# Moving operands read and sums written backwards in all projections, with an offset for each stage

## The chip, the cores and the metric

One core of one Trainium2 chip. The metric is the device time of the whole kernel in microseconds. The kernel before took 1453.62 us (median of three runs, 1452.39 to 1457.54).

## What is computed

Three transformer-like blocks on a sequence of 256 tokens, width 1024, everything in float32. The first block runs retention and a gated linear recurrence side by side, then a gated feed-forward layer of width 3072; each of the two layers of the second part runs a feed-forward layer (width 2816), a mixer (gated linear attention, convolution, windowed attention) and a second feed-forward layer. Cut to what takes the time, the projections:

```python
proj = h @ w_in[l]                                     # 1024 x 8192
y_a = (o * silu(g_ret)) @ w_ret_o[l]                   # 1024 x 1024
y_b = (hl * gelu(y_lru)) @ w_lru_o[l]                  # 1024 x 1024
x = x + mix @ w_out[l]                                 # 1024 x 1024
up = h @ ffn_w_up[l]                                   # 1024 x 6144
x = x + (gelu(gate) * val) @ ffn_w_down[l]             # 3072 x 1024
# and for each of two layers, twice a feed-forward layer and once the mixer:
h = (silu(h @ w_gate) * (h @ w_up)) @ w_down           # 1024 x 2816 twice, 2816 x 1024
p = h @ w_in                                           # mixer, 1024 x 2064
h = concatenate([o_gla, o_conv, o_swa]) @ w_out        # 1024 x 1024
```

## The kernel before

**Splitting.** Each float32 operand of a projection is split into two parts of type fp32r: ScalarE copies the rounded high part, VectorE subtracts it and writes the low part. A product is then three matmuls into the same sums: high by high, high by low, low by high. fp32r matmuls take one column per step; other matmuls in the kernel (transposes, attention, convolution taps) are full float32.

**Weights.** They come in 240 units of 1 MB (128 partitions x 2048 values) through three slots: SyncE issues the loads into `raw`, ScalarE writes `w_hi` (L632), VectorE writes `w_lo` (L1028), TensorE uses both. A slot is filled anew when its unit has been split and split anew when TensorE has used it.

**Activations.** The projections' other operand lies in `a_pair` or `b_pair`: one stretch of 2 x 8 x 256 values per partition, high part first, low part behind it, with 128 values to spare. `operand_pair` (L223) takes the pair out of that stretch from a column `at`, which the tables `A_AT` and `B_AT` (L130, L131) give for each stage: `N_IN` the first input projections, `N_LRU` the recurrence's output projection, `N_UP1` the first up projection, `N_F`, `N_L + 1`, `N_L + 2`, `N_L + 4` the four feed-forward layers of the second part, `N_L` and `N_L + 3` the two mixers; `B_RG` the block-diagonal gates, `B_RETO` the retention's output projection, `B_OUT` the first block's output projection, `B_MIX` the mixers' output projections. A column is 4 bytes. The down projections read `h_hi` and `h_lo` instead, which no table moves.

**Two widths.** `feature_major` (and `token_major`, for one unit of each mixer) issues matmuls of 256 moving columns: in `feature_major` the moving operand is the activation and the stationary one 128 x 128 of the weights, 48 matmuls for each unit. `wide_pass` and `deep_pass` issue matmuls of 512 moving columns: the moving operand is the weights, the stationary one 128 x 128 of the activation. Feature-major are the first block's input projections (but the values), gates, retention and recurrence outputs and the up projection, and most of the mixers' input projections; all else is wide.

**Order.** TensorE's program is written out by hand: unit after unit, with small work (transposes, scores, variances) put between or inside them. Each matmul instruction brings its own weight load, which runs beside the matmul before it. All matmuls go through the helper `mm` (L1713), so they have one line in the profile; sums go to PSUM banks named `stream`, `psm` and `ps7` (shown as `ps`).

Of the kernel before, what the change touches and what calls it, by code (L numbers as in the profile page):

```python
# [26 lines left out]
TT = T // P  # L27
D = 1024
KT = D // P
# [97 lines left out]
(N_LRU, N_IN, N_UP1, N_F, N_L) = (-2, -1, 0, 1, 2)  # L127
NORMS = N_L + 3 * LAYERS
B_RG, B_RETO, B_OUT, B_MIX = range(4)
A_AT = {N_IN: 4, N_LRU: 16, N_UP1: 16, N_F: 0, N_L: 16, N_L + 1: 0, N_L + 2: 0, N_L + 3: 16, N_L + 4: 0}  # L130
B_AT = {B_RG: 16, B_RETO: 16, B_OUT: 0, B_MIX: 0}  # L131


def root_count(i, post, t):
# [69 lines left out]
def build(nc, io, out):  # L204
    with ExitStack() as ctx:  # L205
# [30 lines left out]
        a_hi, a_lo = a_tiles(N_IN)  # L236
        raw = [sb(f"raw{s}", [P, KT, UC]) for s in range(NS)]
        w_hi = [sb(f"w_hi{s}", [P, KT, UC], F32R) for s in range(NS)]
        w_lo = [sb(f"w_lo{s}", [P, KT, UC], F32R) for s in range(NS)]
# [148 lines left out]
        def y_bank(t, n):  # L388

            return psm[:, 2 * t + n, :]  # L390
# [1317 lines left out]
        def _(pe):  # L1708
            passed = {"n": 0}
            a_hi, a_lo = a_tiles(N_IN)  # L1710

            def mm(dst, lhs, rhs, start, stop):
                return nc.tensor.matmul(dst, lhs, rhs, start=start, stop=stop, skip_group_check=True)  # L1713

            def split_unit(c):
                pe.wait_ge(w_split, c + 1)

# [6 lines left out]
            def feature_major(s, dst, tiles, hi_t, lo_t, first, last, kts=range(KT), ready=None):  # L1724

                for n, (lhs, at) in enumerate(tiles):  # L1730
                    for k in kts:
                        if ready and n == 0:
                            ready(k)
                        to = dst[:, at:at + T]
                        begin, end = first and n == 0 and k == kts[0], last and n == len(tiles) - 1 and k == kts[-1]
                        mm(to, lhs(w_hi[s], k), hi_t[:, k, :], begin, False)
                        mm(to, lhs(w_hi[s], k), lo_t[:, k, :], False, False)
                        ins = mm(to, lhs(w_lo[s], k), hi_t[:, k, :], False, end)
                return ins

            def block_cols(f):
# [4 lines left out]
            def token_major(s, dst, col, width, at, begin, a_hi, a_lo, tiles=range(TT), ready=None):  # L1746

                for t in tiles:
                    to = dst[:, at + t * width:at + t * width + width]
                    tok = slice(t * P, t * P + P)  # L1750
                    for k in range(KT):
                        w = slice(col, col + width)
                        if ready:
                            ready(k)
                        mm(to, a_hi[:, k, tok], w_hi[s][:, k, w], begin and t == 0 and k == 0, False)
                        mm(to, a_lo[:, k, tok], w_hi[s][:, k, w], False, False)
                        ins = mm(to, a_hi[:, k, tok], w_lo[s][:, k, w], False, t == TT - 1 and k == KT - 1)
                return ins

            def wide_pass(c, t, dst, hi_t, lo_t, ks, first, last, ready=None):  # L1760

                split_unit(c)
                tok = slice(t * P, t * P + P)
                h, l = wide(w_hi[c % NS]), wide(w_lo[c % NS])
                for n, k in enumerate(ks):
                    if ready:
                        ready(k)
                    begin, end = first and n == 0, last and n == len(ks) - 1
                    mm(dst, hi_t[:, k, tok], h[:, n, :], begin, False)
                    mm(dst, hi_t[:, k, tok], l[:, n, :], False, False)  # L1770
                    ins = mm(dst, lo_t[:, k, tok], h[:, n, :], False, end)
                end_pass(ins, c, t)

            def deep_pass(c, t, hi_t, lo_t, ks, first, last, ready, between):

                split_unit(c)
                tok = slice(t * P, t * P + P)
                h, l = deep(w_hi[c % NS]), deep(w_lo[c % NS])
                for n in range(2):
                    cols = slice(512 * n, 512 * n + 512)  # L1780
                    for j, k in enumerate(ks):
                        if (n, t) == (0, 0):
                            ready(k)
                        mm(y_bank(t, n), hi_t[:, k, tok], h[:, j, cols], first and j == 0, False)
                        mm(y_bank(t, n), hi_t[:, k, tok], l[:, j, cols], False, False)
                        ins = mm(y_bank(t, n), lo_t[:, k, tok], h[:, j, cols], False, last and j == 1)
                        if n + j == 2:
                            end_pass(ins, c, t)
                        elif last and (n, j) == (0, 1):
                            ins.then_inc(half_done, 1)  # L1790
                        if between[2 * n + j]:
                            between[2 * n + j]()
# [33 lines left out]
            for k in range(KT):  # L1826
                for t in range(TT):
                    at = (k % 2) * T + t * P
                    ins = nc.tensor.transpose(psm[:, k // 2, at:at + P], x_t[:, t, k * P:k * P + P], ident)
# [21 lines left out]
            for u in range(8):  # L1851
                if u < 4:
                    project(u, u, stream[u % 3], a_hi, a_lo, (lambda k: pe.wait_ge(a_split, k + 1)) if u == 0 else None)
                else:
                    n, m = divmod(u - 4, 2)
# [418 lines left out]
```

## Time and profile before

| | |
|---|---|
| median of three runs | 1453.62 us |
| the profiled execution's own time | 1452.81 us |
| its span, first to last instruction | 1450.9 us |
| TensorE matmul busy | 1423.1 us (98%), 8888 matmuls |
| weight loads busy | 1247.8 us, 8888 loads |
| VectorE, ScalarE, GpSimd busy | 968.7, 735.9, 94.5 us |
| granted TensorE clock, mean | 0.998 |
| DMA | 259 MB, 179 GB/s |

Times in the profile are microseconds unless marked ns. PE is TensorE's matmuls, PEld its weight loads, DVE is VectorE, ACT ScalarE, POOL GpSimd. A group of instructions reads: line, engine, operation, output <- inputs, sizes (stationary rows * columns, moving partitions x columns), count, then busy time and the mean duration of one in ns, then the idle time of the engine just before them and who ended it. Busy time is a union, so overlapping matmuls count once. The ends of matmuls are modelled; their starts are recorded, so the distance between starts is the sure number.

### The profile page before, as it was taken

Reading aid. Unit: us, or ns where it says so; the run is one execution under the profiler, and the core shown is the slowest. Engines: PE = TensorE matmul, PEld = TensorE weight load, DVE = VectorE, ACT = ScalarE, POOL = GpSimd, SP = SyncE. Lnnn points to the kernel's source line nnn. Section 1 sums busy time; section 2 is a strip of 40 time slices with the busy share of each in tenths; the row PEclk is TensorE's granted clock in tenths of the full one; section 3 lists DMA queues with packets and bytes.
Section 4 is the critical chain, followed back from the end, with each engine's and each line's share of the span. In section 5 each row is a group of like instructions: output and inputs, shape, how many; then the busy total and the mean of one; then the engine's idle time right before and its main releaser. Section 6 shows DMA issues by size and latency. Waiting matters only on the chain. (4 is left out here: it accounts for less than half of the span.)

```text
span 1450.9 us, 21310 instructions
## 1 busy us (share of the span) xinstructions
PE 1423.1 (98%) x8888; PEld 1247.8 (86%) x8888; DVE 968.7 (67%) x1165; ACT 735.9 (51%) x936; POOL 94.5 (7%) x107
## 2 busy tenths in 40 slices
PE   7999999999999999999999999999999999999998
PEld 7899999899988788888987888878888898788886
DVE  5968786688864665546977665556665579665644
ACT  5534854555643544446656444454444567544442
POOL 0001000000000000001720000000000045000000
PEclk9999999999999999999999999999999999999999
DMA  7745455667655666456334755547754462466542
GB/s 244 232 139 182 158 191 198 176 191 201 198 192 163 211 210 224 153 193 159 133 114 143 221 174 189 189 146 246 231 186 171 140 174 103 138 198 197 178 161 101
DMA packets 251411, 259.13 MB, mean 179 GB/s; under 512 B 26659, under 2 KB 213428, under 8 KB 251316
## 3 DMA queue, kind: packets, MB, share of 16 engines
q1 hardware_dynamic: 250432, 255.49, 55.5%
q10 hardware_dynamic: 884, 2.28, 0.4%
q8 instruction: 70, 1.15, 0.3%
q14 instruction: 25, 0.20, 0.0%
HBM read 256.69 MB, written 1.05 MB: 178 GB/s over the span
## 5 line engine op out<-in xcount | busy, mean ns | idle before, releaser
L1028 DVE TENSOR_TENSOR w_lo<-raw,w_hi 128x2048 fp32r<-128x2048 f32 x240 | 548.2, 2287 | 317.5 <-ACT w_hi L632 317.1
L632 ACT ACTIVATE w_hi<-raw 128x2048 fp32r<-128x2048 f32 x240 | 456.3, 1902 | 332.0 <-PE psm L1713 150.8
L1713 PE MATMUL stream<-a_pair,w_hi 128*128 128x256 f32 x2144 | 378.2, 280 | 3.5 <-DVE a_pair L1047 1.9
L1713 PE MATMUL stream<-w_hi,a_pair 128*128 128x512 f32 (+1 forms) x1152 | 363.4, 388 | 8.1 <-DVE w_lo L1028 5.7
L1713 PEld LDWEIGHTS stream<-a_pair,w_hi 128*128 128x128 f32 x2144 | 325.9, 188 | 6.1 <-issue 3.3
L1713 PE MATMUL stream<-a_pair,w_lo 128*128 128x256 f32 x1072 | 298.4, 278 | 0.0
L1713 PEld LDWEIGHTS stream<-w_hi,a_pair 128*128 128x128 f32 x1152 | 214.2, 188 | 53.2 <-DVE w_lo L1028 8.3
L1713 PE MATMUL stream<-w_lo,a_pair 128*128 128x512 f32 (+1 forms) x576 | 221.0, 384 | 0.0
L1713 PEld LDWEIGHTS stream<-a_pair,w_lo 128*128 128x128 f32 x1072 | 201.8, 188 | 0.0
L1713 PE MATMUL psm<-w_hi,h_hi 128*128 128x512 f32 x448 | 175.1, 391 | 0.0
L1713 PE MATMUL psm<-w_hi,h_lo 128*128 128x512 f32 x448 | 174.4, 389 | 0.0
L1713 PE MATMUL psm<-w_lo,h_hi 128*128 128x512 f32 x448 | 174.3, 389 | 0.0
L1713 PEld LDWEIGHTS stream<-w_lo,a_pair 128*128 128x128 f32 x576 | 108.3, 188 | 20.1
L1713 PE MATMUL ps<-w_hi,a_pair 128*128 128x512 f32 x320 | 105.5, 391 | 0.0
L1713 PEld LDWEIGHTS psm<-w_hi,h_lo 128*128 128x128 f32 x448 | 84.1, 188 | 17.6
L1713 PEld LDWEIGHTS psm<-w_lo,h_hi 128*128 128x128 f32 x448 | 84.1, 188 | 17.3
L1713 PEld LDWEIGHTS psm<-w_hi,h_hi 128*128 128x128 f32 x448 | 84.1, 188 | 17.1
L552 POOL TENSOR_TENSOR rs<-var,mhalf 128x1 f32<-128x1 f32 x28 | 15.2, 544 | 1135.8 <-DVE var L1074 1104.5
L1713 PEld LDWEIGHTS ps<-w_hi,a_pair 128*128 128x128 f32 x320 | 60.1, 188 | 12.4
L856 ACT ACTIVATE gu<-stream,rs 128x256 f32<-128x256 f32 x68 | 32.2, 474 | 72.8 <-PE stream L1713 72.8
L1713 PE MATMUL psm<-w_hi,b_pair 128*128 128x512 f32 x192 | 63.0, 398 | 1.1 <-DVE b_pair L1035 1.1
L1713 PE MATMUL ps<-w_lo,a_pair 128*128 128x512 f32 x160 | 62.3, 389 | 0.0
(278 smaller groups left out, 1361.0 us busy)
## 6 DMA issues: line engine op xcount, KB each, us to landing
raw<-in_ffn_w_up SPq DMA_DIRECT2D x136, 512.0 KB, 5.0
raw<-in_ffn_w_down SPq DMA_DIRECT2D x104, 512.0 KB, 4.4
raw<-in_ffn_w_gate SPq DMA_DIRECT2D x88, 512.0 KB, 4.0
raw<-in_w_in SPq DMA_DIRECT2D x80, 512.0 KB, 4.7
raw<-in_w_out SPq DMA_DIRECT2D x24, 512.0 KB, 4.3
raw<-in_w_ret_o SPq DMA_DIRECT2D x8, 512.0 KB, 4.5
raw<-in_w_lru_o SPq DMA_DIRECT2D x8, 512.0 KB, 4.3
diag<-in_conv_diag SPq DMA_DIRECT2D x8, 512.0 KB, 5.8
```

What stands on the lines that cost most here:

```text
L552: nc.gpsimd.tensor_tensor(to, of, mhalf[:, 0:1].broadcast_to([P, n]), ALU.pow).then_inc(rstd_ready, 1)
L632: nc.scalar.activation(w_hi[s][:, :, 0:n], raw[s][:, :, 0:n], ACT.Copy).then_inc(w_hi_ready, 1)
L856: nc.scalar.activation(th_t[:, 2 * (g % 2) + t, :], up_bank(g, t)[:, 0:UC], ACT.Tanh, scale=rs4[:, 2 + t:3 + t]).then_inc(th_ready, 1)
L1028: V.tensor_tensor(w_lo[s][:, :, 0:n], raw[s][:, :, 0:n], w_hi[s][:, :, 0:n].bitcast(F32), ALU.subtract).then_inc(w_split, 1)
L1713: return nc.tensor.matmul(dst, lhs, rhs, start=start, stop=stop, skip_group_check=True)
```

## The change

It adds a helper, `backward`, which hands `mm` the output and the moving operand with their columns in reverse order; the stationary operand stays as it is. The four functions that issue projections call it for each of their three matmuls. Since the moving operand and the sums are both reversed, each sum lands where it did. The two tables of offsets get new values. Nothing else differs.

```diff
-A_AT = {N_IN: 4, N_LRU: 16, N_UP1: 16, N_F: 0, N_L: 16, N_L + 1: 0, N_L + 2: 0, N_L + 3: 16, N_L + 4: 0}
-B_AT = {B_RG: 16, B_RETO: 16, B_OUT: 0, B_MIX: 0}
+A_AT = {N_IN: 32, N_LRU: 64, N_UP1: 48, N_F: 16, N_L: 16, N_L + 1: 32, N_L + 2: 48, N_L + 3: 8, N_L + 4: 24}
+B_AT = {B_RG: 16, B_RETO: 40, B_OUT: 64, B_MIX: 0}
...
+            def backward(to, of, moving, begin, end):
+
+                return mm(to[:, ::-1], of, moving[:, ::-1], begin, end)
+
...
-                        mm(to, lhs(w_hi[s], k), hi_t[:, k, :], begin, False)
-                        mm(to, lhs(w_hi[s], k), lo_t[:, k, :], False, False)
-                        ins = mm(to, lhs(w_lo[s], k), hi_t[:, k, :], False, end)
+                        backward(to, lhs(w_hi[s], k), hi_t[:, k, :], begin, False)
+                        backward(to, lhs(w_hi[s], k), lo_t[:, k, :], False, False)
+                        ins = backward(to, lhs(w_lo[s], k), hi_t[:, k, :], False, end)
...
-                    mm(dst, hi_t[:, k, tok], h[:, n, :], begin, False)
-                    mm(dst, hi_t[:, k, tok], l[:, n, :], False, False)
-                    ins = mm(dst, lo_t[:, k, tok], h[:, n, :], False, end)
+                    backward(dst, hi_t[:, k, tok], h[:, n, :], begin, False)
+                    backward(dst, hi_t[:, k, tok], l[:, n, :], False, False)
+                    ins = backward(dst, lo_t[:, k, tok], h[:, n, :], False, end)
```

`token_major` and `deep_pass` are changed in the same way.

## Rows read from the trace of the kernel before

**Rows 1.** The page: busy us by engine, share of the span, instructions.
```profile
PE 1423.1 (98%) x8888; PEld 1247.8 (86%) x8888; DVE 968.7 (67%) x1165; ACT 735.9 (51%) x936; POOL 94.5 (7%) x107
```

**Rows 2.** The page, granted TensorE clock in tenths, the span in 40 slices.
```profile
PEclk9999999999999999999999999999999999999999
```

**Rows 3.** Waits, whole span: who waited for whom, total us, times, longest.
```profile
ACT w_hi L632 <- PE psm L1713: 150.8, 51, 4.4
ACT w_hi L632 <- PE stream L1713: 114.0, 36, 6.3
...
ACT w_hi L632 <- PE ps L1713: 53.8, 20, 3.5
...
PE stream L1713 <- DVE w_lo L1028: 6.3, 10, 1.3
```

**Rows 4.** Groups of matmuls by form, whole span; first and last of each width.
```profile
L1713 PE MATMUL stream<-a_pair,w_hi 128*128 128x256 f32 x2144 | 378.2, 280 | 3.5 <-DVE a_pair L1047 1.9 <-DVE a_pair L1066 1.1 <-DVE w_lo L1028 0.6
L1713 PE MATMUL stream<-w_hi,a_pair 128*128 128x512 f32 x1088 | 351.9, 394 | 5.7 <-DVE w_lo L1028 5.7
...
L1713 PE MATMUL psm<-w_lo,a_pair 128*128 128x512 f32 x32 | 12.6, 395 | 0.0
...
L1713 PE MATMUL stream<-w_lo,a_pair 128*128 128x256 f32 x32 | 8.9, 279 | 0.0
```

**Rows 5.** Groups by form, 280 to 400 us, the first up projection.
```profile
L1713 PE MATMUL stream<-a_pair,w_hi 128*128 128x256 f32 x708 | 120.5, 276 | 0.0
L1713 PE MATMUL stream<-a_pair,w_lo 128*128 128x256 f32 x354 | 97.7, 276 | 0.0
```

**Rows 6.** Groups by form, 99 to 122 us, the first input projections.
```profile
L1713 PE MATMUL stream<-a_pair,w_hi 128*128 128x256 f32 x133 | 23.4, 279 | 0.0
L1713 PE MATMUL stream<-a_pair,w_lo 128*128 128x256 f32 x67 | 18.7, 278 | 0.0
```

**Rows 7.** Timeline of matmuls in a mixer: start us, length us, what, count.
```profile
689.91 0.28 PE L1713 MATMUL stream<-a_pair,w_lo 128*128 128x256 f32 x1
...
690.97 0.28 PE L1713 MATMUL stream<-a_pair,w_lo 128*128 128x256 f32 x1
```

**Rows 8.** Groups by form, 1405 to 1445 us, the last down projection.
```profile
L1713 PE MATMUL psm<-w_lo,h_hi 128*128 128x512 f32 x60 | 23.3, 389 | 0.0
L1713 PE MATMUL psm<-w_hi,h_lo 128*128 128x512 f32 x59 | 23.0, 389 | 0.0
L1713 PE MATMUL psm<-w_hi,h_hi 128*128 128x512 f32 x59 | 23.0, 389 | 0.0
```

**Rows 9.** Timeline of matmuls, the first stage of 512 columns.
```profile
60.25 0.39 PE L1713 MATMUL psm<-w_lo,a_pair 128*128 128x512 f32 x1
...
61.65 0.39 PE L1713 MATMUL psm<-w_lo,a_pair 128*128 128x512 f32 x1
```

**Rows 10.** Timeline of matmuls around a pause in the first input projections.
```profile
123.27 0.28 PE L1713 MATMUL stream<-a_pair,w_lo 128*128 128x256 f32 x1
...
125.36 0.28 PE L1713 MATMUL stream<-a_pair,w_lo 128*128 128x256 f32 x1
125.99 1.05 PE L1713 MATMUL ps<-keep,sq 128*128 128x1 f32 x8 [0.35 <-POOL sq L569]
...
127.23 0.28 PE L1713 MATMUL stream<-a_pair,w_lo 128*128 128x256 f32 x1
...
128.93 0.28 PE L1713 MATMUL stream<-a_pair,w_lo 128*128 128x256 f32 x1
```

**Rows 11.** The page, weight loads of the largest group.
```profile
L1713 PEld LDWEIGHTS stream<-a_pair,w_hi 128*128 128x128 f32 x2144 | 325.9, 188 | 6.1 <-issue 3.3
```

**Rows 12.** Timeline of matmuls, convolution taps in full float32.
```profile
731.77 2.11 PE L1713 MATMUL ps<-up,diag 128*128 128x256 f32 x9
```

## What I expect, and why

> **What bounds the kernel now.** I read the busy times first: TensorE is busy 1423.1 of 1450.9 us, VectorE 968.7 [rows 1]. Then the clock: every slice of the span has the full grant, so all durations below are at 2.4 GHz [rows 2]. Then who waits for whom. The dearest wait of TensorE's matmuls is 6.3 us in all, for the low half of a weight unit, while ScalarE waits 150.8, 114.0 and 53.8 us for TensorE to free a weight slot [rows 3]. So nothing feeds TensorE late: the kernel is a chain of matmuls, and the change acts on the matmuls alone. What counts is no instruction's duration (these overlap and their ends are modelled) but the distance from one start to the next.
>
> The projections come in two widths: 3600 matmuls of 256 moving columns, in six groups, and 3840 of 512, in eleven; the first and the last group of each width are shown [rows 4]. At one column per cycle they would take 3600 x 106.7 ns = 384 us and 3840 x 213.3 ns = 819 us. I get the real distances by counting matmuls in a stretch that holds nothing else (the length plus one duration, over the count, since matmuls that reach into the stretch are counted):
> - the first block's up projection: (120 + 0.276) us / (708 + 354) = 113.3 ns [rows 5]
> - the input projections, g_ret and y_lru: (23 + 0.279) / (133 + 67) = 116.4 ns [rows 6]
> - the mixer: nine matmuls from 689.91 to 690.97, 117.8 ns [rows 7]
> - down projections, 512 columns: (40 + 0.389) / (59 + 59 + 60) = 226.9 ns [rows 8]
> - the first stage's 512 columns: six matmuls from 60.25 to 61.65, 233.3 ns [rows 9].
>
> Two losses are to be seen. **One is everywhere and goes with the columns:** 113.3 and 226.7 ns are 272 and 544 cycles, 17 for every 16 columns. **The other comes and goes:** 3 to 5 ns on a 256 matmul, 6.6 ns on a 512 one in the first stage. It isn't set by addresses alone. The first block's up projection and the mixer read their operand at the same offset (16) and differ by 4.5 ns. And in one stage at one offset the distance changes at a pause: 18 matmuls from 123.27 to 125.36 stand 116.1 ns apart, then eight matmuls of one column come in, and the 15 from 127.23 to 128.93 are 113.3 apart [rows 10]. So it depends on where two streams stand to each other in time. The second stream is the weight load: there is one for every matmul (2144 loads for the 2144 of that group), 188 ns long [rows 11], beside the running matmul.
>
> **The change, part by part.** It adds and removes no instruction, no wait and no transfer. The queues of SyncE, ScalarE, VectorE and GpSimd keep their order; ScalarE and VectorE write operand tiles of the same sizes, from 32 bytes before to 256 bytes behind their old places. (1) All 7440 projection matmuls read their moving operand from the last column down; (2) they write PSUM in the same descending order, so what lands is the same; (3) the operand pair starts at another offset in ten of the thirteen stages; the block-diagonal gates (16), the first mixer's projections (16) and the mixers' output projections (0) keep theirs. The 256-wide passes have the operand pair as moving side, the 512-wide ones as stationary side, so an offset shifts one stream against the other in both.
>
> *Cost of reading and writing downward.* No row shows a matmul that does this. Bound below: the loss per 16 columns goes. The nearest row is the convolution's taps, full float32, which take two cycles per column and show no such loss: (2.11 - 0.38) us / 8 = 216.3 ns for 256 columns, 3 ns over 2 x 106.7 [rows 12]. By them 512 columns would take 213.3 + 3 = 216.3 and 256 columns 109.7. That is at most 3840 x (226.9 - 216.3) = 41 us and, from a mean of (1152 x 113.3 + 2448 x 116.9) / 3600 = 115.7 ns, 3600 x 6.0 = 22 us: -63 us in all. Bound above: the two cycles per column of those same rows, if a downward stream is not served at one column per cycle: 3840 x (429 - 227) + 3600 x (216 - 116) = +1136 us. I take zero: the loss is the same 1 in 16 for both widths, whatever the roles and however much of the matmul the 188 ns load covers, so it looks like a property of the stream itself, and nothing in the rows gives a stream a preferred direction.
>
> *Worth of the offsets and of the direction against the weight load.* This acts on the second loss. Of the 3600 matmuls, 24 units x 48 = 1152 are the up projection, already at 113.3. The other 2448 stand between 113.3 and 117.8; I take 116.9 for them, the middle of the slow rows (116.1 to 117.8) [rows 6, 7, 10]. If all reach 113.3: 2448 x 3.6 = 8.8 us. The first stage's 96 wide matmuls: 96 x (233.3 - 226.7) = 0.6 us. Sum -9.4 us. If nothing changes: 0. If it turns out worse, see the third rival. I take the whole -9.4: each slow stage gets another offset or at least, with the direction, another meeting of its two streams, two streams that run the same way pass over each other more slowly than two that meet, and the low value is one that every kind of 256 stage is seen to reach. That is a choice, not a derivation.
>
> *What is late next.* A PE that is 9 us faster over the whole asks for each weight unit under 1% sooner; ScalarE's 318.6 us of waiting for slots [rows 3] hides that. Even the 63 us of the lower bound fit: it is 5 to 6% on each unit. I let 5 us return as waits in that case.
>
> **Sum.** The profiled execution took 1452.8 us, span 1450.9 plus 1.9 around it; the median of the three timed ones is 1453.6, 0.8 above. 1452.8 - 9.4 = 1443.4; I say 1443.
>
> **The rules of the Trainium skill.** The skill's page TensorE: Matmul & The Clock Gate, section Back-to-back issue gap, gives N/2.4 + 2.5 ns. The 227 and 113 ns of rows 5 and 8 disagree with it, the measurement decides for this kernel; by the rule the wide matmuls would be at 215.8, which is the first rival's result. The same page (Step-by-step) says that PE has two independent SBUF read ports, so a weight load takes no bandwidth from the running matmul. By that rule the offsets do nothing and the sum is 0; rows 10, with 116.1 and 113.3 ns on either side of a pause, speak against it without proving that the port is the cause. The page Advanced Engine Details and Errata, section PSUM Cachelines, speaks against this change: any non-contiguous pattern slows matmuls significantly, and two consecutive elements should be contiguous. Descending neighbours are still neighbours, so I hold it unlikely; if the hardware counts them as non-contiguous, the last rival follows. No row here has a stepped PSUM write.
>
> **The rivals.**
> 1. *The 1 in 16 goes as well.* For it: the taps, which stream at half the rate beside the same loads, don't have it [rows 12], and the extra cycles are whole multiples of 16 (16, 32, and 48 in the first stage's 233.3), as if the load's passes were counted too. Against it: half of a 512 matmul lies beyond its load, and still has its share. It gives 1452.8 - 63 + 5, less or more as it goes in part: 1390 to 1430, most likely 1395.
> 2. *Nothing changes by direction or offset*, or gains in some stages pay for losses in others: 1447 to 1460.
> 3. *Two streams in the same direction stay on each other.* They part at half the speed of the moving one, so where they meet they meet for longer. Place: every weight load. Price: the wide stages, now without the second loss, get the first stage's 233.3: 3744 x 6.4 = 24 us; the up projection gets 117.8: 1152 x 4.5 = 5 us; +29 us, 1482. It decides once a quarter of the wide matmuls (1140 x 6.4 = 7.3 us) is hit with nothing gained elsewhere. For it: the up projection and the wide stages stand at their best now, and can only lose.
> 4. *A downward stream or write isn't served at full rate*: from +5% up to the +1136 us above, about 2590.
>
> **How the numbers follow.** Forecast (1438 to 1447) 0.34, of which 0.06 is a gain under 0.5%. Rival 1: 0.21. Rival 2: 0.20. Rival 3: 0.17, of which 0.02 within 0.5%. Rival 4: 0.08. A measurement of this kernel tells about 0.5% (7 us) from no change. Faster 0.28 + 0.21 = 0.49; same 0.06 + 0.20 + 0.02 = 0.28; slower 0.15 + 0.08 = 0.23. For the range I leave out rival 4 (0.08), the far part of rival 1 (0.06) and of rival 3 (0.04): 1392 to 1484. The forecast's own range is 1438 to 1447.
>
> **What would show it.** In the changed profile: the same 8888 matmuls; the up projection still with 1062 matmuls in 120 us, the down projections with 178 in 40 us; the mixer's nine matmuls in 1.02 us, not 1.06; the first stage's six in 1.36, not 1.40. If 1 in 16 goes, the 40 us hold 187 wide matmuls. If streams stay on each other, 173. A mean matmul duration of 276 or 389 ns that grows by 3 to 6 is the second loss. The prediction is wrong if the wide stages, 3840 matmuls that I leave untouched, move by more than 1 ns each.

## The result: about 2% slower

The changed kernel takes 1483.72 us (median of three runs, 1482.76 to 1485.72) against 1453.62: a ratio of 1.020, 95% interval 1.0176 to 1.0223. So it is slower for sure; whether by more or less than 2% stays open. The forecast was 1443. In the later comparisons the kernel before had 36 executions with medians of 1457.5 to 1458.5 us, four of them under 1454; beside 1458.4 the changed kernel is 1.7% slower. The profiled execution took 1485.72 us, with a span of 1483.9.

Busy times and granted clock, from the page of the changed kernel (compare [rows 1, 2]):

```profile
PE 1458.3 (98%) x8888; PEld 1262.3 (85%) x8888; DVE 968.6 (65%) x1165; ACT 736.6 (50%) x936; POOL 94.0 (6%) x107
...
PEclk9999999999999999999999999999999999999999
```

Only TensorE grew: 1458.3 against 1423.1 us, 35.2 more, for a span 33.0 longer. The clock is the same in every slice. The waits of ScalarE for a weight slot (compare [rows 3]; total us, times, longest) grew with it, so TensorE is still the engine that everything waits for:

```profile
ACT w_hi L632 <- PE psm L1713: 163.4, 53, 4.4
ACT w_hi L632 <- PE stream L1713: 119.5, 37, 6.5
```

The distances, by the same counting as before. Groups by form in 290 to 410 us, the first up projection (compare [rows 5]):

```profile
L1713 PE MATMUL stream<-a_pair,w_hi 128*128 128x256 f32 x668 | 120.3, 282 | 0.0
L1713 PE MATMUL stream<-a_pair,w_lo 128*128 128x256 f32 x335 | 94.5, 282 | 0.0
```

(120 + 0.282) / (668 + 335) = 119.9 ns, where it was 113.3. In 100 to 123 us, the first input projections (compare [rows 6]):

```profile
L1713 PE MATMUL stream<-a_pair,w_hi 128*128 128x256 f32 x129 | 23.3, 283 | 0.0
L1713 PE MATMUL stream<-a_pair,w_lo 128*128 128x256 f32 x65 | 18.4, 283 | 0.0
```

(23 + 0.283) / 194 = 120.0 ns, where it was 116.4. The first mixer, timeline of matmuls (start us, length us; compare [rows 7]):

```profile
709.79 0.28 PE L1713 MATMUL stream<-a_pair,w_lo 128*128 128x256 f32 x1
...
710.87 0.28 PE L1713 MATMUL stream<-a_pair,w_lo 128*128 128x256 f32 x1
```

Nine matmuls in 1.08 us, 120.0 ns apart, where it was 117.8. The last down projection, 1430 to 1470 us (compare [rows 8]):

```profile
L1713 PE MATMUL psm<-w_hi,h_lo 128*128 128x512 f32 x58 | 23.0, 397 | 0.0
L1713 PE MATMUL psm<-w_hi,h_hi 128*128 128x512 f32 x58 | 23.0, 397 | 0.0
L1713 PE MATMUL psm<-w_lo,h_hi 128*128 128x512 f32 x57 | 22.6, 397 | 0.0
```

(40 + 0.397) / 173 = 233.5 ns, where it was 226.9. And the first stage of 512 columns (compare [rows 9]):

```profile
60.80 0.40 PE L1713 MATMUL psm<-w_lo,a_pair 128*128 128x512 f32 x1
...
61.51 0.40 PE L1713 MATMUL psm<-w_lo,a_pair 128*128 128x512 f32 x1
```

Three matmuls in 0.71 us, 236.7 ns, where it was 233.3.

So no stage gained. In the down projections 226.7 to 233.3 ns is 544 to 560 cycles, in the up projection 113.3 to 120.0 is 272 to 288: 16 cycles for each matmul. The other stages rose by less.

The bill, from the mean distance of neighbouring starts in every stage of both traces: the wide matmuls rose from 227.5 to 233.4 ns on average, 3840 x 5.9 = 22.7 us; the up projection gives 1152 x 6.7 = 7.7 us; the other 2448 matmuls of 256 columns rose by 2.2 ns on average, 5.4 us. Together 35.8 us, and the busy time grew by 35.2. Least moved the retention's output projection (116.7 to 117.8), the recurrence's (117.8 to 118.3) and the second mixer (117.3 to 117.8).

### The profile page after: what moved, and what is told of

It reads as the page before. It is cut to its first block and busy times, and to the rows that moved or that the text cites. A ratio compares the mean times of both kernels' runs of the same rounds, so it can differ in the third digit from the quotient of the medians.

```text
span 1483.9 us, 21310 instructions
## 1 busy us (share of the span) xinstructions
PE 1458.3 (98%) x8888; PEld 1262.3 (85%) x8888; DVE 968.6 (65%) x1165; ACT 736.6 (50%) x936; POOL 94.0 (6%) x107
## 5 line engine op out<-in xcount | busy, mean ns | idle before, releaser
L1713 PE MATMUL stream<-a_pair,w_hi 128*128 128x256 f32 x2144 | 390.0, 284 | 2.8 <-DVE a_pair L1047 1.5
L1713 PE MATMUL stream<-w_hi,a_pair 128*128 128x512 f32 (+1 forms) x1152 | 370.2, 394 | 7.5 <-DVE w_lo L1028 5.2
L1713 PEld LDWEIGHTS stream<-a_pair,w_hi 128*128 128x128 f32 x2144 | 330.5, 188 | 5.1 <-issue 2.9
L1713 PE MATMUL stream<-a_pair,w_lo 128*128 128x256 f32 x1072 | 303.1, 283 | 0.0
L1713 PE MATMUL stream<-w_lo,a_pair 128*128 128x512 f32 (+1 forms) x576 | 224.9, 390 | 0.0
L1713 PE MATMUL psm<-w_hi,h_hi 128*128 128x512 f32 x448 | 178.7, 399 | 0.0
L1713 PE MATMUL psm<-w_lo,h_hi 128*128 128x512 f32 x448 | 178.1, 397 | 0.0
L1713 PE MATMUL psm<-w_hi,h_lo 128*128 128x512 f32 x448 | 178.0, 397 | 0.0
```

## The experiments

The runs e3 to e15 are one execution each, and executions of one kernel lie up to 9 us apart here, so in them the distances between starts count and not the time. A count of matmuls in 40 us is good to one matmul, 1.3 ns. Where a mean over a whole stage is given, it is that of the distances of neighbouring starts.

Each edit is given against the changed kernel, whose helper is `backward`, unless it says otherwise. "Offsets of before" means the two tables of the kernel before.

### Direction or offsets?

Theory D: the direction costs 16 cycles, at any offset. Theory O: the new offsets cost.

```diff
 e1_down_old_offsets
-A_AT = {N_IN: 32, N_LRU: 64, N_UP1: 48, N_F: 16, N_L: 16, N_L + 1: 32, N_L + 2: 48, N_L + 3: 8, N_L + 4: 24}
-B_AT = {B_RG: 16, B_RETO: 40, B_OUT: 64, B_MIX: 0}
+A_AT = {N_IN: 4, N_LRU: 16, N_UP1: 16, N_F: 0, N_L: 16, N_L + 1: 0, N_L + 2: 0, N_L + 3: 16, N_L + 4: 0}
+B_AT = {B_RG: 16, B_RETO: 16, B_OUT: 0, B_MIX: 0}
```

> Everything as in the changed kernel, but with the offsets of the kernel before. If the direction alone costs (theory D: 16 cycles more for each weight load, at any offset): 512-column matmuls 233.3 ns apart, 256-column ones 120.0, time 1480 to 1490. If the new offsets cost (theory O): 226.7 and 113 to 118 ns, time within 5 us of the kernel before. A mixture: some stages at 227, some at 233.

Measured: 1487.25 us, ratio 1.0204 (1.0182 to 1.0226) to the kernel before beside it. The down projections hold 173 matmuls in 40 us, 233.5 ns, the up projection 1002 in 120, 120.0 ns. With the old offsets the whole loss is there: theory D, but for one stage. The first stage's wide matmuls, at offset 4, stand 233.3 ns apart in e1 (six from 60.19 to 61.59 us), as in the kernel before. Where the ascending matmul stood at 233.3 already, the direction adds nothing; it is no fixed surcharge.

```diff
 e2_up_new_offsets (against the kernel before)
-A_AT = {N_IN: 4, ...
-B_AT = {B_RG: 16, ...
+A_AT, B_AT of the changed kernel
```

> Ascending as in the kernel before, with the new offsets. Theory D: down projections 226.7 ns, up projection of the first block 113.3, the first stage's wide matmuls 226.7 (offset 32 columns in place of 4), time 1448 to 1458. Theory O: 1480 to 1490, 233.3 and 120.0 ns.

Measured: 1466.35 us, ratio 1.0061 (1.0040 to 1.0082). Up and down projections as D wants (113.3 and 226.9 ns). But not everything: the time lies over D's 1458, and the first stage's wide matmuls, expected at 226.7, have a mean of 232.4. Timeline of the first feed-forward layer of the second part, whose stationary operand went from offset 0 to 16:

```profile
521.42 0.40 PE L1713 MATMUL ps<-w_lo,a_pair 128*128 128x512 f32 x1
...
522.12 0.39 PE L1713 MATMUL ps<-w_lo,a_pair 128*128 128x512 f32 x1
```

Three matmuls in 0.70 us: 233.3 ns, ascending. In the kernel before the same stage stood at 226.7 (six from 519.70 to 521.06). Here only the stationary operand has moved, the moving one (the weights) lies where it lay. So an ascending matmul can be brought to the descending one's distance by a bad offset, and the new offsets cost 0.6% of their own. In the changed kernel they add nothing to the direction: e1 isn't faster than the changed kernel, and this stage, at the same offset 16, stands at 233.3 there too (six from 520.62 to 522.02).

### The read or the write?

Theory R: the descending read costs; theory W: the descending write.

```diff
 e3_read_down_only
-                return mm(to[:, ::-1], of, moving[:, ::-1], begin, end)
+                return mm(to, of, moving[:, ::-1], begin, end)
 e4_write_down_only
-                return mm(to[:, ::-1], of, moving[:, ::-1], begin, end)
+                return mm(to[:, ::-1], of, moving, begin, end)
```

> The moving operand is read from the last column down, the sums are written upward, so the columns of each output stand in the wrong order; all else as in the changed kernel. If the descending read costs (theory R, a meeting of two SBUF reads): 233.3 and 120.0 ns, 1480 to 1490 us. If the descending write to PSUM costs (theory W): 226.7 and 113 to 118 ns, about 1454 us. If both are needed: in between.

Measured: 1482.85 us in one execution. Down projections, groups by form in 40 us:

```profile
L1713 PE MATMUL psm<-w_hi,h_lo 128*128 128x512 f32 x58 | 23.1, 397 | 0.0
L1713 PE MATMUL psm<-w_hi,h_hi 128*128 128x512 f32 x58 | 23.1, 397 | 0.0
L1713 PE MATMUL psm<-w_lo,h_hi 128*128 128x512 f32 x58 | 23.0, 397 | 0.0
```

(40 + 0.397) / 174 = 232.2 ns (one matmul more or less in the count is 1.3 ns; the mean over the stage is 233.3). The up projection holds 682 + 340 matmuls in 120 us, 117.7 ns, where the changed kernel has 119.9 at the same offset. That is 2.5 us, within the 3 us that the changed kernel's own executions span, so it isn't shown that the downward write has a part in it.

> The opposite: read upward, written downward, output columns in the wrong order. Theory R: 226.7 and 113 to 118 ns, about 1454 us. Theory W: 233.3 and 120.0 ns, 1480 to 1490 us.

Measured: 1463.42 us, beside 1466.35 for e2, which has the same offsets and writes upward. The same 40 us:

```profile
L1713 PE MATMUL psm<-w_hi,h_hi 128*128 128x512 f32 x60 | 23.4, 389 | 0.0
L1713 PE MATMUL psm<-w_lo,h_hi 128*128 128x512 f32 x59 | 23.0, 389 | 0.0
L1713 PE MATMUL psm<-w_hi,h_lo 128*128 128x512 f32 x59 | 23.0, 389 | 0.0
```

(40 + 0.389) / 178 = 226.9 ns. In the up projection (120 + 0.276) / (707 + 354) = 113.4 ns. The read pays for the wide matmuls, and the write alone costs nothing at either width.

### Is it the weight load beside it?

Theory L: the cost comes from the load, by its columns. Theory S: once per descending matmul. Theory M, on the ascending loss: it goes with the moving columns. All four have the offsets of before.

```diff
 e5_up_64_weights, e6_down_64_weights (n = 128 for the first matmul into its sums, 64 for the others)
-                return mm(to[:, ::-1], of, moving[:, ::-1], begin, end)
+                return mm(to[0:n, :], of[:, 0:n], moving, begin, end)                 # e5
+                return mm(to[0:n, ::-1], of[:, 0:n], moving[:, ::-1], begin, end)     # e6
 e7_up_one_weight, e8_down_one_weight
+                return mm(to, of[:, 0:1].broadcast_to([P, P]), moving, begin, end)                     # e7
+                return mm(to[:, ::-1], of[:, 0:1].broadcast_to([P, P]), moving[:, ::-1], begin, end)   # e8
```

> Ascending, offsets of before; every projection matmul but the first into its sums takes only 64 of the 128 stationary columns, so half of the rows of sums stay unfinished. The weight loads are half as long, the moving columns as many. If the loss of 1 in 16 belongs to the moving columns (theory M): 512 columns still 226.7 ns apart, 256 columns 113.3. If it is caused by the weight loads (theory L, 32 cycles for each load of 128 beside a 512-column matmul and 16 beside a 256-column one): half of it, 220.0 and 110.0 ns.

> Descending read and write, offsets of before, 64 of the 128 stationary columns as in the run beside it. Against that run: if the descending read pays 16 cycles for each load of 128 columns, by the columns loaded (theory L), the extra halves to 8 cycles, 3.3 ns: 230.0 ns under theory M for the rest. If it pays 16 cycles once per matmul, however short the load (theory S, a start-up cost of a descending stream): 6.7 ns, 233.3 and 120.0 ns.

Measured: e5 1464.34 us, e6 1481.15. In e5 the loads take 134 ns in place of 188 and the down projections' matmuls stand *further* apart, 176 in 40 us: (40 + 0.392) / 176 = 229.5 ns, and the up projection's too, (120 + 0.278) / 1031 = 116.7. Neither theory had that. In e6, 40 us of the down projections:

```profile
L1713 PE MATMUL psm<-w_lo,h_hi 128*64 128x512 f32 x58 | 23.0, 396 | 0.0
L1713 PE MATMUL psm<-w_hi,h_lo 128*64 128x512 f32 x57 | 22.6, 396 | 0.0
L1713 PE MATMUL psm<-w_hi,h_hi 128*64 128x512 f32 x56 | 22.2, 396 | 0.0
L1713 PE MATMUL psm<-w_hi,h_hi 128*128 128x512 f32 x2 | 0.8, 398 | 0.0
```

(40 + 0.396) / 173 = 233.5 ns: the full descending distance with half the load. Not theory L. The up projection, though, is at (120 + 0.282) / 1016 = 118.4 ns, not at theory S's 120.0.

> Ascending, offsets of before; the stationary operand is one column repeated 128 times, so the weight load has its full length but stays at one address in each partition (the sums are those of that column). Control for the next run. Theory M: 226.7 and 113.3 ns. If the weight load's sweep over addresses causes the loss of 1 in 16: fewer, towards 216 and 109 ns.

> The same with the descending read and write. If the extra comes from two streams that sweep SBUF the same way (my third rival's mechanism): the extra 6.7 ns is gone or changed, 226.7 and 113 to 117 ns. If it belongs to the descending read itself (theory S): 233.3 and 120.0 ns as in the changed kernel.

Measured: e7 1466.84 us, e8 1480.16. e7, ascending, the load at one address, 40 us of the down projections:

```profile
L1713 PE MATMUL psm<-w_hi,h_lo 128*128 128x512 f32 x58 | 22.9, 394 | 0.0
L1713 PE MATMUL psm<-w_hi,h_hi 128*128 128x512 f32 x58 | 22.9, 394 | 0.0
L1713 PE MATMUL psm<-w_lo,h_hi 128*128 128x512 f32 x58 | 22.9, 394 | 0.0
```

(40 + 0.394) / 174 = 232.2 ns (the mean over that stage is 231.7), and the up projection is at (120 + 0.278) / 1031 = 116.7: theory M misses both. The same stage of e8, descending, then its up projection:

```profile
L1713 PE MATMUL psm<-w_hi,h_lo 128*128 128x512 f32 x58 | 23.0, 397 | 0.0
L1713 PE MATMUL psm<-w_hi,h_hi 128*128 128x512 f32 x58 | 23.0, 397 | 0.0
L1713 PE MATMUL psm<-w_lo,h_hi 128*128 128x512 f32 x57 | 22.6, 397 | 0.0
```

```profile
L1713 PE MATMUL stream<-a_pair,w_hi 128*128 128x256 f32 x681 | 120.4, 279 | 0.0
L1713 PE MATMUL stream<-a_pair,w_lo 128*128 128x256 f32 x341 | 95.1, 279 | 0.0
```

(40 + 0.397) / 173 = 233.5 and (120 + 0.279) / 1022 = 117.7 ns. For 512 columns the descending distance is the same with a whole load, half a load and a load that doesn't move. The ascending one changes with each: 226.9, 229.5, 232.2. So what the load does matters to an ascending matmul, and beside its own ascending control the direction costs 6.6, 4.0 and 1.3 ns: what is constant is the distance of 560 cycles, not the extra. For 256 columns the descending distance itself changes with the load: 120.0 in e1, which has the same offsets, 118.4 and 117.7, and the means of the other 256-column stages go the same way (119.7 to 120.0 in e1, 118.3 to 118.9 in e6, 117.8 to 118.1 in e8). There theory S fails.

### Columns and the order of blocks

Theory S again (16 cycles once), theory C: the extra goes by columns. Then, whether the cost lies in the order of columns inside 64 bytes or in the order of the blocks; these two write upward.

```diff
 e9_up_384, e10_down_384 (offsets of before; n = all columns for the first matmul into its sums, 3/4 of them for the others)
+                return mm(to[:, 0:n], of, moving[:, 0:n], begin, end)                       # e9
+                return mm(to[:, 0:n][:, ::-1], of, moving[:, 0:n][:, ::-1], begin, end)     # e10
 e11_blocks_down, e12_inside_down (offsets of before)
+                m = moving.rearrange("p (a b) -> p a b", b=16)
+                return mm(to, of, m[:, ::-1, :], begin, end)      # e11
+                return mm(to, of, m[:, :, ::-1], begin, end)      # e12
```

> Ascending, offsets of before; every projection matmul but the first into its sums moves three quarters of its columns (384 of 512, 192 of 256), the rest of the sums stays unfinished. If the ascending loss goes by columns (1 in 16): 384 columns take 384 x 17/16 = 408 cycles = 170.0 ns. If it is a fixed 32 cycles per matmul: 416 cycles = 173.3 ns.

> Descending read and write, three quarters of the columns as in the run beside it. If the descending read adds 16 cycles once per matmul (theory S): 408 + 16 = 424 cycles, 176.7 ns. If it adds by columns (1 in 32, so 3 in 32 in all; theory C): 384 x 35/32 = 420 cycles, 175.0 ns. 256-column form, now 192: S gives 204 + 16 = 220 cycles, 91.7 ns; but there the weight load of 107 ns is longer and should set the distance, so this form tells little.

Measured: 1282.32 and 1283.80 us. With a quarter of the columns gone TensorE waits for VectorE here and there, so I read the distances inside a down projection, six matmuls each. e9:

```profile
569.81 0.33 PE L1713 MATMUL psm<-w_hi,h_hi 128*128 128x384 f32 x1
...
570.85 0.33 PE L1713 MATMUL psm<-w_hi,h_hi 128*128 128x384 f32 x1
```

1.04 us / 6 = 173.3 ns, 416 cycles: 32 over the 384 columns, as many as for 512. e10:

```profile
565.90 0.34 PE L1713 MATMUL psm<-w_hi,h_hi 128*128 128x384 f32 x1
...
566.97 0.34 PE L1713 MATMUL psm<-w_hi,h_hi 128*128 128x384 f32 x1
```

1.07 / 6 = 178.3 ns, 428 cycles (the mean over the stages is 177.8, 427 cycles): 10 to 12 more than ascending. Both of my figures for e10 were built on 408 and miss; against the measured 416, S would be 432 and C 428. C fits better, but 256 columns also pay 16, so neither is a law. The narrower form, 192 columns, stands at 112.0 ns in either direction, (20 + 0.274) / 181 from 300 to 320 us in e9 and (120 + 0.275) / 1074 from 280 to 400 us in e10: here the direction costs nothing. What falls for sure is my loss of 1 in 16: it is 32 cycles at 512 and at 384 columns and 16 at 256.

> Ascending write, offsets of before; the moving operand is read in blocks of 16 columns (64 bytes), the last block first, upward inside each block. If the cost sits in the step from one column to the one below it inside a block: none here, 226.7 ns. If it sits in the step from a block to the one before it, or in where the matmul starts reading: 233.3 ns. A jump of 31 columns after every 16 may have a price of its own, then over 233.3.

> The other way round: blocks of 16 in ascending order, each read from its last column down. If the cost sits inside the blocks: 233.3 ns. If it sits in the order of blocks or in the start at the far end: 226.7 ns.

Measured: e11 1485.03 us, 233.5 ns in the down projections and (120 + 0.284) / 1002 = 120.0 ns in the up projection: all of the descending cost, with every 16 columns read upward. Whether it is the order of the blocks or the jump from each to the next that costs, this run can't tell. e12 1639.26 us, the slowest of all:

```profile
1599.72 0.43 PE L1713 MATMUL psm<-w_hi,h_hi 128*128 128x512 f32 x1
...
1601.32 0.43 PE L1713 MATMUL psm<-w_hi,h_hi 128*128 128x512 f32 x1
```

Six matmuls in 1.60 us, 266.7 ns, 640 cycles: one extra cycle for every four columns, in either width (133.4 ns for 256, 320 cycles). But not in every stage. The first input projections of e12, whose operand starts at offset 4, 16 bytes past a multiple of 64, in 100 to 123 us:

```profile
L1713 PE MATMUL stream<-a_pair,w_hi 128*128 128x256 f32 x130 | 23.4, 281 | 0.0
L1713 PE MATMUL stream<-a_pair,w_lo 128*128 128x256 f32 x64 | 18.0, 281 | 0.0
```

(23 + 0.281) / 194 = 120.0 ns. So the high price hangs on where the blocks start in SBUF: 133.3 ns in all the 256-column stages at offset 16, 117 to 120 in the only one at 4. Elsewhere the price of the plain descending read is that of its blocks' order; the order inside them costs nothing when the blocks descend too, and much when they ascend.

### One descending matmul among ascending ones, and a moving operand that doesn't move

```diff
 e13_one_of_three_down (against the kernel before; the third matmul of each three)
-                        ins = mm(to, lhs(w_lo[s], k), hi_t[:, k, :], False, end)
+                        ins = mm(to[:, ::-1], lhs(w_lo[s], k), hi_t[:, k, ::-1], False, end)
 e14_up_one_column (offsets of before)
+                return mm(to, of, moving[:, 0:1].broadcast_to([P, moving.shape[1]]), begin, end)
 e15_down_at_4
+A_AT = {N_IN: 4, N_LRU: 12, N_UP1: 4, N_F: 2, N_L: 20, N_L + 1: 6, N_L + 2: 12, N_L + 3: 28, N_L + 4: 40}
+B_AT = {B_RG: 12, B_RETO: 4, B_OUT: 20, B_MIX: 0}
```

> Offsets of before; of each three matmuls only the third reads and writes downward. If each descending matmul pays its own 16 cycles: the mean of three is 226.7 + 6.7/3 = 228.9 ns for 512 columns, time about 1466. If the cost sits in the change from one matmul's stream to the next (the place where one read ends and the next begins), two of three changes now differ from both pure kernels: up to 231 to 233 ns, time 1475 or more.

Measured: 1465.62 us. Groups by form, 40 us of the down projections; the third of three is the one from `h_lo`:

```profile
L1713 PE MATMUL psm<-w_hi,h_lo 128*128 128x512 f32 x59 | 23.4, 396 | 0.0
L1713 PE MATMUL psm<-w_hi,h_hi 128*128 128x512 f32 x59 | 23.0, 390 | 0.0
L1713 PE MATMUL psm<-w_lo,h_hi 128*128 128x512 f32 x59 | 23.0, 389 | 0.0
```

(40 + 0.392) / 177 = 228.2 ns, and the mean duration is 396 ns for the descending ones beside 390 and 389 for the others. Each descending wide matmul pays by itself, 6 to 7 ns by the durations; the changes of direction cost nothing to be seen. The up projection doesn't follow: (120 + 0.28) / (681 + 341) = 117.7 ns, two thirds of the way from 113.3 to 120.0 with one matmul of three descending. As this stage takes 117.7 in some ascending kernels too (e18 below), the run can't say what one such matmul costs there.

> Ascending write, offsets of before; the moving operand is one column repeated, so the moving read stays at one address (the sums are those of that column). If the 32 cycles that even an ascending 512-column matmul loses come from the moving read's way through SBUF: near 213.3 + 3 = 216 ns, as the convolution taps suggest. If they come with any fp32r matmul: 226.7 ns.

Measured: 1400.17 us. Down projections, groups by form in 35 us, then the up projection in 120 us:

```profile
L1713 PE MATMUL psm<-w_hi,h_lo 128*128 128x512 f32 x55 | 20.8, 379 | 0.0
L1713 PE MATMUL psm<-w_hi,h_hi 128*128 128x512 f32 x55 | 20.8, 379 | 0.0
L1713 PE MATMUL psm<-w_lo,h_hi 128*128 128x512 f32 x54 | 20.5, 379 | 0.0
```

```profile
L1713 PE MATMUL stream<-a_pair,w_hi 128*128 128x256 f32 x718 | 120.3, 275 | 0.0
L1713 PE MATMUL stream<-a_pair,w_lo 128*128 128x256 f32 x359 | 98.7, 275 | 0.0
```

(35 + 0.379) / 164 = 215.7 ns and (120 + 0.275) / 1077 = 111.7 ns. With the moving operand read at one place, the wide matmul's loss of 32 cycles is down to 6. And the loss that comes and goes is gone: every stage stands at 215.7 to 215.9 or at 111.7 ns, by its width, whatever its offset. Both losses need a moving read that moves. The 111.7 ns are, to 0.3 ns, the distance of 192 columns in e9 and e10; so in this run something other than the columns sets it. The weight load is the likely one, but no run shows it.

> Descending as in the changed kernel, with offsets that aren't multiples of 8 columns (2, 4, 6, 12, 20, 28; one at 40). If no offset helps a descending read, as the nine offsets tried so far suggest: every wide stage at 233.3 ns or above, 1480 to 1490 us. If the offsets were the missing piece (a phase difference that is no multiple of 8): at least one up stage at 226.7 ns.

Measured: 1487.15 us, 233.5 ns in the down projections; 233.3 or more in every wide stage and 119 to 120 ns in every 256-column stage. No offset tried frees the descending read.

### Offsets for the ascending kernel

```diff
 (against the kernel before; B_MIX stays at 0)
 e16_up_at_64   every entry of A_AT and B_AT 64
 e17_up_48      N_IN, N_LRU, N_UP1, N_L, N_L + 3, B_RG, B_RETO: 48, the others 0
 e18_up_16      the same entries 16, the others 0
```

> Ascending, every operand pair at offset 64 but the mixers' output projection (0). Ascending wide stages stood at 227 ns at offset 0 and 64 and at 229 to 234 at 4, 16, 24, 32, 48. If multiples of 64 columns (256 bytes) are the good places: all wide stages 226.7, the first one too (-0.6 us). The 256-column stages: 113.3 to 118 ns, unknown at 64 (the recurrence's output stood at 120.0 there). Time within 6 us of the kernel before, either way.

Measured: 1465.20 us, ratio 1.0049 (1.0035 to 1.0064). Wide matmuls of the first stage, timeline:

```profile
60.66 0.39 PE L1713 MATMUL psm<-w_lo,a_pair 128*128 128x512 f32 x1
...
61.34 0.39 PE L1713 MATMUL psm<-w_lo,a_pair 128*128 128x512 f32 x1
```

Three in 0.68 us, 226.7 ns, down from 233.3 at offset 4, as expected. But the up projection, 290 to 400 us:

```profile
L1713 PE MATMUL stream<-a_pair,w_hi 128*128 128x256 f32 x612 | 110.2, 283 | 0.0
L1713 PE MATMUL stream<-a_pair,w_lo 128*128 128x256 f32 x307 | 86.9, 283 | 0.0
```

(110 + 0.283) / 919 = 120.0 ns at offset 64, ascending. The place that suits a stationary operand is the worst seen for a moving one. Both bounds of the expectation were missed: 120.0 for 118, and 6.8 us for 6.

> Ascending; every stage of 256-column matmuls at offset 48, every wide stage but the first at 0. The first up projection stood at 113.3 ns at 16 and at 48, at 120.0 at 64. If the offset decides: all 256-column stages near 113.3, the 2448 slow ones gain up to 3.6 ns each, 1446 to 1452. If the stage's history decides, as at the pause in the kernel before: a mixture of 113 to 120 and a time within 6 us of the kernel before.

Measured: 1450.80 us, ratio 0.9951 (0.9936 to 0.9965): the best kernel of this study, 0.5% faster than the kernel before and 2.2% than the changed one. A piece of the first mixer:

```profile
699.98 0.28 PE L1713 MATMUL stream<-a_pair,w_lo 128*128 128x256 f32 x1
...
700.66 0.28 PE L1713 MATMUL stream<-a_pair,w_lo 128*128 128x256 f32 x1
```

Six matmuls in 0.68 us, 113.3 ns, where it was 117.8 at offset 16. The up projection holds (120 + 0.276) / 1061 = 113.4 ns. The means over the whole of the two mixers are 114.3 and 114.6, where they were 117.3. The first block's input projections and gates stay at 116 to 118, its retention and recurrence outputs at 117.8. So it is a mixture: the offset alone doesn't decide.

> The same with 16 in place of 48, which differs from the kernel before in the first input projections alone (16 for 4). If the offset decides: those 1152 matmuls go from 117 to 113.3 ns, -4 us. If history decides: 116 to 118 ns, no change that can be measured.

Measured: 1458.29 us, ratio 1.000 (0.999 to 1.001). The up projection, which has its old offset, 280 to 400 us:

```profile
L1713 PE MATMUL stream<-a_pair,w_hi 128*128 128x256 f32 x681 | 120.4, 279 | 0.0
L1713 PE MATMUL stream<-a_pair,w_lo 128*128 128x256 f32 x341 | 95.1, 279 | 0.0
```

(120 + 0.279) / 1022 = 117.7 ns, at the same offset at which the kernel before has 113.3: for 1152 x 4.4 = 5 us. The two kernels differ in nothing but the offset of an earlier stage, but it isn't shown that this offset is the cause. All ten executions of e18 took 1457.5 to 1459.1 us, and so, to 0.4 us, did thirteen of the fourteen of the kernel before beside them; the fourteenth took 1452.2, like the profiled one. So more likely most executions of the kernel before have the up projection at 117.7 too, and the stage takes one distance or the other by something that changes between executions. That is argued: none of the slower ones was profiled. It would also account for e17's gain: 5 us in the up projection and 816 x 2.9 = 2.4 us in the mixers are the 7.5 us between the medians, while between the two profiled executions there are 2.4.

## Why the prediction was wrong

**What bounds the kernel** was right: the clock, the waits and the other engines are as they were, and the change went one to one into the time.

**The step that failed** is the cost of reading downward, "I take zero", with its reason that "nothing in the rows gives a stream a preferred direction". A downward read brings a matmul of 512 columns to 560 cycles, 16 more than the 544 at which the wide stages stood, and one of 256 to 283 to 288, where the up projection stood at 272. That is the whole loss, or nearly: e1 has it at the old offsets. The sum had zero. The nearest row in the trace, the convolution taps, was a bound from below; no row showed a downward read, and the rows could not say zero either.

**The second term, -9.4 us**, had the wrong sign. The 2448 matmuls were to come to 113.3 ns and went to 118 to 120. That I gave the direction credit for "another meeting of its two streams" had no row behind it. That credit takes the load to run upward, the third rival takes it to run downward, and no row shows which it does. That the distance can come down in a slow stage is seen in e17 (the mixers at 114.3 and 114.6), but with an ascending read and at another offset than the change's, in one profile. And the sum started from 1452.8 us, while most executions of the kernel before took about 1458.

**The loss of "1 in 16"** was a reading of two widths that happened to be in the ratio 2 to 1. e9 gives 32 cycles at 384 columns as at 512, so it doesn't go with the columns. My argument for taking zero, that a loss so regular must be a property of the stream, rested on it. That it is the moving read's is right for 512 columns (e14), that direction doesn't matter to it doesn't follow. At 256 columns most of it is not: with a standing read 111.7 of the 113.3 ns are left.

**The write** was costed right, at nothing (e4). The rule of the Trainium skill against this change (Advanced Engine Details and Errata, PSUM Cachelines: a non-contiguous pattern slows matmuls) doesn't reach it: descending neighbours cost nothing here, 226.9 ns. **The ports**: the Trainium skill (TensorE: Matmul & The Clock Gate, Step-by-step) says that the two reads are independent. e2 doesn't bear that out: the stationary operand's place alone, 0 or 16 columns, moved the wide matmul from 226.7 to 233.3 ns; that the ports are where the two meet isn't shown. **The rule N/2.4 + 2.5 ns** of the Trainium skill (the same page, Back-to-back issue gap) is met by 512 columns where the moving read stays at one address: 215.7 ns measured, 215.8 by the rule. By the rule 256 columns would take 109.2 ns, an estimate; measured were 111.7.

**The third rival** gave 1482 us and the measured time is 1484, by its very prices: wide stages to 233.3. Yet its mechanism isn't what the runs show for the wide matmuls. Two streams that stay on each other would have to notice a load of half the length or one that doesn't move; e6 and e8 stand at 233.5 like the changed kernel. For 256 columns it isn't excluded: there the descending distance changes with the load (120.0 in e1, 118.4 in e6, 117.7 in e8). And it put the up projection at 117.8, which is 119.9. The near number is luck as far as the wide matmuls go: it came from a row of a bad case, not from the story beside it. (Its "quarter of the wide matmuls", 1140, is 30% of the 3840.) The range, 1392 to 1484, ended at that number; it should have reached a little over it.

**What stays open**: why the order of 64-byte blocks (or the jumps between them) and their start matter to the moving read, how the ascending read comes to lose between 16 and 48 cycles by its and the load's addresses, and what picks 113.3 or 117.8 at one offset in one kernel. A stationary operand handed over in reverse order wasn't tried.

## What to carry to other kernels

Where TensorE is full, measure the distance between matmul starts in cycles and compare it with the columns; a few per cent over can be the operands' reads (with a moving read that stays at one address 226.9 ns became 215.7 here), and where the tiles begin in SBUF changes them. Let the moving operand ascend through memory without breaks; the write to PSUM may run either way. Try offsets for the moving and the stationary role apart (here 48 columns did best for the up projection and the mixers' moving tiles, 0 or 64 for stationary ones), and judge an offset by the times of many executions, because one stage at one offset stood at 113.3 ns in one profile and at 117.7 in another.

## What the hardware showed that I had not expected

- A descending moving read puts wide matmuls 560 cycles apart (233.3 ns), with a whole load, half a load or one at a single address, and at almost every place of the stationary operand (the first stage at offset 32 took 236.6). An ascending one stands between 226.7 and 234 by those same things. Where it is at 233.3 already, descending costs nothing more. At 384 columns it costs 10 to 12 cycles, at 192 nothing.
- Blocks of 16 columns that ascend, read backwards inside, cost a cycle for every four columns (266.7 ns for 512), 96 cycles more than the ascending read; a fully descending one costs 16 more. With the blocks starting 16 bytes off a multiple of 64 that price was gone: 120.0 ns in place of 133.4 for 256 columns.
- A shorter weight load made ascending matmuls slower: 229.5 against 226.9 ns.
- fp32r matmuls of 512 columns stand 215.7 ns apart if the moving read stays at one address: the whole kernel then takes 1400 us, beside 1458 for the kernel before.
